# One transfer of 16 KB a partition, in place of two of 8 KB, for each block of expert weights

## The reference

```python
N_EXPERTS = 8
TOP_K = 2
D_FF_EXPERT = 3584

def _swiglu(x, w1, w3, w2):
    return (jax.nn.silu(x @ w1) * (x @ w3)) @ w2

def moe_swiglu(x, w_router, b_router, w1, w3, w2):
    logits = (x @ w_router).astype(jnp.float32) + b_router.astype(jnp.float32)
    top_vals, top_idx = lax.top_k(logits, TOP_K)
    top_w = jax.nn.softmax(top_vals, axis=-1)
    gates = jnp.sum(jax.nn.one_hot(top_idx, N_EXPERTS, dtype=jnp.float32) * top_w[..., None], axis=-2)
    out = jnp.zeros_like(x)
    for e in range(N_EXPERTS):
        out = out + gates[..., e:e + 1].astype(x.dtype) * _swiglu(x, w1[e], w3[e], w2[e])
    return out
```

## Time and profile before

| | |
|---|---|
| time, median of 3 runs | 2306.05 us (2303.07 to 2315.46) |
| profiled execution: span from the first to the last instruction (no other time of it is given) | 2306.0 us |
| PE busy | 2204.6 us, 96% |
| DVE busy | 1502.4 us, 65% |
| ACT busy | 980.5 us, 43% |
| POOL busy | 346.0 us, 15% |
| moved by DMA | 552.20 MB, mean 239 GB/s over the span |
| packets of DMA, all queues | 176770, of them 133280 under 8 KB |
| transfers of expert weights | 336 of 1024.0 KB |
| stage of the experts, by PE's products | 839 to 1799 us |

### The profile page before, as it was taken

The page is one execution under the profiler, slowest core; times in us unless marked ns, Lnnn a source line. Parts: engine busy times, 40 slices in busy tenths (PEclk is TensorE's granted clock), DMA queues, the critical chain, the costliest instruction groups (busy, mean ns, idle before and its releaser), DMA issues.

```text
span 2306.0 us, 29557 instructions
## 1 busy us (share of the span) xinstructions
PE 2204.6 (96%) x11972; PEld 1870.1 (81%) x11972; DVE 1502.4 (65%) x1489; ACT 980.5 (43%) x1043; POOL 346.0 (15%) x95
## 2 busy tenths in 40 slices
PE   8999999989999979999999999999999798969999
PEld 7777899989777868888888888888888586648998
DVE  4342677755333568898888898988889301445776
ACT  0133210010133257777777777778776203241000
POOL 1001200000001112322323223223243000100000
PEclk9999999999999989999999999999999996979999
DMA  9532578643513459999999999999999332303530
GB/s 341 183 124 73 170 268 294 237 132 115 180 60 110 165 209 381 372 384 367 384 367 384 366 385 371 385 374 380 384 387 343 132 135 84 110 0 110 183 128 19
DMA packets 176770, 552.20 MB, mean 239 GB/s; under 512 B 11264, under 2 KB 98944, under 8 KB 133280
## 3 DMA queue, kind: packets, MB, share of 16 engines
q1 hardware_dynamic: 167984, 516.77, 60.9%
q10 hardware_dynamic: 6912, 24.97, 2.7%
q0 software_dynamic: 1776, 9.08, 1.0%
HBM read 527.19 MB, written 23.59 MB: 239 GB/s over the span
## 4 chain that ended last, share of the span: by engine, by line
PE 90%; DVE 6%; ACT 2%; issue 1%; DMA 1%; POOL 0%; DVEq 0%; SPq 0%; ACTq 0%; POOLq 0%
PE act_ps L990 25%; PE act_ps L825 13%; PE dve_ps L1015 12%; PE dve_ps L825 9%; PE dve_ps L918 8%; PE act_ps L918 8%; PE job_ps L951 5%; PE job_ps L825 2%; DVE weights_rest L1884 2%; PE job_ps L877 2%; PE job_ps L998 1%; PE job_ps L888 1%; PE act_ps L1126 1%; ACT expert_short L1414 0%; DVE pre_norm L1673 0%
## 5 line engine op out<-in xcount | busy, mean ns | idle before, releaser
L1884 DVE TENSOR_TENSOR weights_rest<-weight_ring,expert_short 128x2048 fp32r<-128x2048 f32 x280 | 768.2, 2784 | 113.6 <-ACT expert_short L1414 113.6
L1414 ACT ACTIVATE expert_short<-weight_ring 128x2048 fp32r<-128x2048 f32 x336 | 640.8, 1917 | 115.1 <-PE act_ps L990 75.7
L724 POOL TENSOR_TENSOR weights_rest<-weight_ring,expert_short 128x2048 fp32r<-128x2048 f32 x56 | 267.4, 4776 | 685.6 <-ACT expert_short L1414 685.6
L990 PE MATMUL act_ps<-expert_short,tokens_short 128*128 128x512 f32 x896 | 355.1, 396 | 12.0 <-DVE tokens_rest L1894 12.0
L990 PE MATMUL act_ps<-weights_rest,tokens_short 128*128 128x512 f32 x896 | 350.0, 391 | 0.0
L990 PE MATMUL act_ps<-expert_short,tokens_rest 128*128 128x512 f32 x896 | 349.9, 391 | 0.0
L1330 ACT ACTIVATE arena_mla<-act_ps 128x256 f32<-128x256 f32 (+2 forms) x89 | 34.2, 385 | 419.5 <-PE act_ps L918 346.1
L990 PEld LDWEIGHTS act_ps<-expert_short,tokens_short 128*128 128x128 f32 x896 | 168.8, 188 | 46.1 <-issue 12.3
L990 PEld LDWEIGHTS act_ps<-expert_short,tokens_rest 128*128 128x128 f32 x896 | 168.8, 188 | 36.4
L990 PEld LDWEIGHTS act_ps<-weights_rest,tokens_short 128*128 128x128 f32 x896 | 169.0, 189 | 33.7
L1813 DVE TENSOR_TENSOR weights_rest<-weight_ring,ffn_weights_short 128x2048 fp32r<-128x2048 f32 x66 | 151.3, 2293 | 2.3
(11 more groups left out here) (323 smaller groups left out, 3958.3 us busy)
## 6 DMA issues: line engine op xcount, KB each, us to landing
weight_ring<-in_moe_w SPq DMA_DIRECT2D x336, 1024.0 KB, 6.9
weight_ring<-in_w_in SPq DMA_DIRECT2D x44, 1024.0 KB, 7.4
weight_ring<-in_ffn_w SPq DMA_DIRECT2D x32, 1024.0 KB, 7.1
weight_ring<-in_w_out SPq DMA_DIRECT2D x12, 1024.0 KB, 6.9
weight_ring<-in_w_gate SPq DMA_DIRECT2D x11, 1024.0 KB, 5.5
weight_ring<-in_w_up SPq DMA_DIRECT2D x11, 1024.0 KB, 8.0
weight_ring<-in_w_down SPq DMA_DIRECT2D x10, 1024.0 KB, 5.9
weight_ring<-in_w_ple_gate SPq DMA_DIRECT2D x8, 1024.0 KB, 6.8
```

The costliest lines, as they stand in the source:

```text
L724: nc.gpsimd.tensor_tensor(ring_lo[slot][:, half], ring[:, slot, half], shorts[u % SHORTS][:, :], ALU.subtract)\
L990: m = nc.tensor.matmul(bank[0:CAP, :], a[:, 4 * c + k, :], w[:, k, :], start=(c == k == i == 0), stop=(c == 1 and k == 3 and i == 2))
L1414: nc.scalar.activation(shorts[u % SHORTS][:, :], ring[:, slot, half], ACT.Copy).then_inc(moe_w_short, 1)
L1884: V.tensor_tensor(ring_lo[slot][:, half], ring[:, slot, half], shorts[u % SHORTS][:, :], ALU.subtract)\
```

## The change

A block of expert weights is now one transfer of 4096 float32 in each partition. The semaphore of the slot rises by 16 for a block where it rose by 32, and ACT waits for 16 times the number of blocks that the slot has had. All other weights are loaded as before.

```diff
             def load_expert_block(e, b, base):
                 kind, g = MOE_ORDER[b]
-                for c in range(2):
-                    half = slice(c * 2048, (c + 1) * 2048)
-                    sp.dma_start(ring[:, moe_slot(b), half], t[f"moe_{kind}"][e][g][:, half]).then_inc(moe_here[b % SLOTS], 16)
+                sp.dma_start(ring[:, moe_slot(b), :], t[f"moe_{kind}"][e][g]).then_inc(moe_here[b % SLOTS], 16)
...
                 if u % 2 == 0:
-                    act.wait_ge(moe_here[b % SLOTS], 32 * (MOE_TURNS * it + (b // SLOTS + 1)))
+                    act.wait_ge(moe_here[b % SLOTS], 16 * (MOE_TURNS * it + (b // SLOTS + 1)))
```

## The result

The changed kernel takes 2313.8 us (median of 20 runs, 2309.41 to 2322.18), the kernel before 2308.1 us (20 runs, 2303.07 to 2315.46). The ratio is 1.0019, with a 95% interval of 1.0011 to 1.0027: about 4.4 us slower (2.5 to 6.2), within the 0.5% that was forecast as no change, and clear of zero. The medians lie further apart, 5.7 us, because the times are not spread evenly: of the 20 of the kernel before, 13 are 2308.4 us or less and 7 are 2311.5 us or more, with none between; of the 20 of the changed kernel, 3 are 2310.4 us or less and 17 are 2312.6 us or more. The profiled execution has a span of 2312.3 us, 6.3 us over that of before.

A forecast was written before the change was run, and what follows sets the result against it. The prediction took PE to bound the stage of the experts. Its terms were 0 except +1 us for the scatter at the start, added to the 2306.05 us median for 2307 us, range 2298 to 2317 us.

The forecast's parts named there:

- PE bounds the stage: Stage of the experts: PE is waited for, 5.44 us a block, 119.49 us an expert; DMA merely keeps its pace.
- issues: SP's queue in the expert stage: 168 fewer issues save 56 us, covered by waits for PE; value 0.
- wait: ACT before converting a block: waiting for one transfer instead of both halves ends at the same moment; value 0.
- SP's waits: SP's queue before expert transfers: its waits for PE grow by 30 to 60 us.
- The landing: Expert blocks: landing takes 7 to 12 us under 19.4 us of cover before ACT's conversion; value 0.
- The rate: Weight packets in the expert stage: 16 KB takes 0.62 to 0.64 us, under the limit of 0.696; value 0.
- rival B: Steady expert stage: 16 KB packets cost more than two of 8 KB, DMA becomes the bound; 2352 to 2661 us, chance 0.06.
- Rival A: Expert transfers: a fixed cost per transfer is on the path, so fewer are faster; 2295 us, chance 0.06.
- Rival C: Weight transfers: 16 KB rows are cut into two 8 KB packets, so DMA sees no change; 2306 us, chance 0.10.
- The scatter: Last token-row scatter before the first expert: its packets wait behind longer weight packets; +1 us, bounds -5.3 to +2.
- so I add it to the median: Whole kernel: the +1 us sum is added to the three-run median of 2306.05 us, giving 2307 us.
- Other transfers beside the weights: Last expert's gathers and each expert's rows: 3 us more each would move nothing; value 0.

The follow-up runs named there:

- quarters: Kernel before, with each expert block in four transfers of 4 KB a partition instead of two: 2306.34 us, ratio 0.9986.
- the block held for the scatter: Changed kernel, SP holding the first expert's sixth block until the last scatter of token rows has landed: 2305.57 us, ratio 0.9977 to the kernel before.
- held for the rows too: Changed kernel, SP holding the first expert's sixth block until that expert's token rows have been loaded too: 2305.42 us, ratio 0.9978 to the kernel before.
- the two later issues: Changed kernel, SP issuing each block of the stage four or eight units of PE later: ratios 1.0036 and 1.2771 to the kernel before.
- ACT later: Kernel before, no transfer changed, ACT making its first conversion twice: 2313.72 us, ratio 1.0022.
- the seventh block in halves or held: Changed kernel, first expert's seventh block in two transfers, or held until the scatter has landed: ratios 1.0025 and 1.0019 to the kernel before.
- the sixth block held: First expert's sixth block held for the scatter in the changed kernel (0.9977) or kernel before (0.9985), or for token rows too in the changed kernel (0.9978).
- the one with eight units: Changed kernel, SP issuing each block of the stage eight units of PE (21.8 us) later: 2948.98 us, ratio 1.2771 to the kernel before.
- the seventh block joined: Kernel before, with only the first expert's seventh block in one transfer of 16 KB a partition: ratio 1.0001.

## Why the prediction was right, and where it was off

- **The number.** The forecast was 1 us more than the kernel before, and 4.4 us (2.5 to 6.2) were measured. Of the 6.8 us between 2307 and 2313.8 some 2 us are the base: the median of three runs was 2306.05, that of twenty is 2308.1. That 2313.8 us lies between 2298 and 2317 is owed to the 9 us of spread that the range allowed above the median, not to a cost that had been priced: in this the prediction was lucky. What was earned is "no change beyond 0.5%", which rests on the stage being PE's.
- **PE bounds the stage; issues, wait and landing are worth nothing.** Right, and shown: an expert takes 119.48 us, and even an issue 10.9 us later cost only 2.5 us in the stage. The sentence that a landing of over 19 us costs "one to one" was wrong: with that issue a block lands some 20 us after its slot is free, ACT waits 112.5 us for blocks, and the stage is 2.5 us longer, since behind the conversion ACT is also ahead of PE.
- **SP's waits and the DMA share.** SP waits 80 us longer for PE where I forecast 30 to 60. I had counted one issue of 0.333 us less to a block, but a block's two issues take 0.80 us (at 808.61) to 0.88 us, so 0.47 us or more go away with each. The share is 0.96 for a forecast of 0.97 to 0.98. Neither is waited for.
- **The landing.** Forecast at 7 to 8 us, measured 9.5 (7.7 to 11.6). I had added 0.4 us to a median over both halves of the blocks. The second half, which decides, landed later than the first: for the block issued at 1086.11, 6.1 us for the first half and 8.1 for the second. One transfer does not land a block sooner. Nothing hung on it.
- **The rate (rival B).** Refuted. From 1330 to 1332 us the weights' queue moved 0.87 MB in 54 packets at 101.2% of 16 engines, 0.60 us a packet, against the 0.62 to 0.64 that I took and the limit of 0.696. The 12 KB packets were the right row to go by, and the instruction packet was not.
- **Rival A, a fixed cost on the path.** Refuted: an expert is 0.01 us shorter, and the whole is longer. The Trainium skill's rule to coalesce ("SBUF — State Buffer", The DMA setup-cost knee) is stated for DMA-bound transfers. These are not waited for, and here smaller transfers gave the shorter time (0.9986 for quarters).
- **Rival C, the packets stay the same.** Refuted by the packets' count, 143792 for a forecast of about 143800.
- **The scatter.** The mechanism was right and its size was off. I bounded the landing at 2 us later and took +1; it came 2.1 us later, at 817.4, just past the 815 to 817 that I had named. The wait over the 3.9 us of a scatter alone grew from 3.7 to 5.8 us, so by less than the doubling, and the upper end was the value to take. The Trainium skill's rule of turns at packet boundaries ("DMA: Bandwidth & Descriptors", Queues, rings and completion order) gave that end, and the trace agrees (2.1 us for its 2). PE gave back 0.9 us of it, since its 48 products, begun later, were made in 7.61 us instead of 8.54: I had priced the clock for a shorter pause only. In both traces the granted clock is 0.50 from 818 to 822 us and 1.00 from 824 to 828 us, so that products which begin 2.2 us later have less of the lower level. The other bound, 5.3 us sooner with no wait for weights, came close: 4.3 us with the block held for the scatter and 6.0 us with it held for the rows too.
- **The step that did not hold: "so I add it to the median".** I took the 500 us behind the stage as rigid. They are not. The stage itself is: in every profile but those of the two later issues it took 960.5 to 961.7 us. So of some 4.4 us, 1.2 us arise at the start and the rest behind the stage, and in the profiled execution the part behind it grew by 5.6 us, with a lower granted clock in its attention stages. The run with nothing but a delay shows that a delay at that place is enough, and it does not stand alone: the changed kernel, ACT later, and the seventh block in halves or held start 1.0 to 1.4 us later, and the lower ends of their four intervals are 2.1 us or more. The other way nothing is enlarged: starts 4.3 to 6.0 us sooner (quarters, the sixth block held) gave 3.2 to 5.3 us.
- **What the clock has to do with it.** The mean granted clock of a whole execution, averaged over all runs of a kernel, was 0.969 to 0.970 in each kernel that starts later (the one with eight units, 0.890, aside), and 0.971 to 0.973 in the kernel before on all three chips and in each kernel that starts as early or earlier. So the added time goes with the lower clock over many runs. Within the changed kernel it does too: the fastest of the 20 (2309.41 us) had 0.972, the slowest (2322.18) 0.967. One profile can't show it: the part behind the stage took 505.8 us in the kernel before, but 511.3 us with the seventh block joined, where nothing had moved, and 512.5 and 511.2 us in two of the kernels that start earliest. The delay seems to change how often an execution falls into the longer of the two groups of times, more than to move each of them; how it does so is not shown, and stays open, for I did not move the later stages alone.
- **Other transfers beside the weights.** Right: the store and the load of an expert's rows land after 11.1 us, where they took 8.0 and 8.3 (from 1080 to 1200 us), the 3 us that I had put down (over the whole stage the medians are 10.7 and 10.4 us), and nothing waits for them.

## What to carry to other kernels

A change to transfers that are hidden can still cost time, through a small transfer on the chain that shares the DMA engines with them: look for the transfers in the chain of work, see what is beside them, and count the turns by the length of the others' packets. If a bulk transfer is not urgent, hold it back until the small one has landed; here that was worth at least as much (0.9977, 0.9966 to 0.9988) as the best size of the bulk transfers (0.9986, 0.9976 to 0.9997, for quarters). And when an edit is aimed at one transfer of many, look in the trace for the one that moved before believing the time.

## What the hardware showed that I had not expected

- A scatter of 128 rows of 4 KB, on its way with a weight block of 2 MB, took 3.9 us with nothing beside it and 5.8, 7.6 and 9.7 us beside weight packets of 4, 8 and 16 KB. With the same 2 MB beside it, it is the length of the others' packets, or the number of transfers that they come in, that counts.
- The DMA share tells little of what is left. With quarters it was 1.00 at 381 GB/s (900 to 1000 us), with whole blocks 0.96 at 377, at the same pace of PE.
- The end of the program, some 1000 us behind an edit and with no instruction of it changed, took between 504.7 us (sixth block held for the scatter) and 515.1 us (ACT later) in the profiled executions. Of a difference of a few us in this kernel, the part before the stages in which PE pauses can be read from a trace; the part in them only from many runs.
